# A float32 stack of two transformer blocks on one core: the gate product worked in place in PSUM, and the low weights of the split transitions made in smaller pieces and partly by VectorE

## What is computed

```
first block, layer l:
    x += norm(mix(norm(x) @ w_in) @ w_out)            # "a_in", attention, "a_out"
    x += norm((silu(h @ gate) * (h @ up)) @ down)     # h = norm(x): "a_ffn_in", "a_ffn_out"
    e = p[l] @ w_ple_up[l]                            # "a_ple_up"
    g = sigmoid(rmsnorm(x, g_ple_gate[l]) @ w_ple_gate[l])   # "a_gate"
    x += rmsnorm(e * g, g_ple_post[l])                # "a_ple"
second block, layer l:
    x += 0.5 * swiglu(norm(x)); x += mixer(norm(x)); x += 0.5 * swiglu(norm(x))
```

## Time and profile before

| | us |
|---|---|
| median of 3 runs (3408.14 to 3410.47) | 3408.16 |
| the profiled execution's own time | 3410.03 |
| its span | 3408.2 |
| TensorE busy | 3313.7 (97%) |
| GpSimd busy | 1652.4 (48%) |
| VectorE busy | 1194.6 (35%) |
| ScalarE busy | 1171.9 (34%) |
| mean granted TensorE clock, of full | 0.986 |

### The profile page before, as it was taken

One profiled execution on the slowest core, in us unless ns is written; L12 is line 12 of the kernel. 1 busy time (PEld: TensorE's weight loads), 2 busy tenths in 40 slices (PEclk: granted clock), 3 DMA queues, 4 the chain that ended last, 5 costly groups with the idle time before them and its releaser, 6 DMA issues.

```text
span 3408.2 us, 44206 instructions
## 1 busy us (share of the span) xinstructions
PE 3313.7 (97%) x16096; PEld 2741.6 (80%) x16096; DVE 1194.6 (35%) x1882; ACT 1171.9 (34%) x1848; POOL 1652.4 (48%) x894
## 2 busy tenths in 40 slices
PE   8999999999999999899999999999999999799998
PEld 6788888787788887888888788888888888588887
DVE  4534124445441144511344332124311433421133
ACT  4743222438442233422233432222322333232222
POOL 6735444567264445644447344444544453154443
PEclk9999999999999999999999999999999999899998
DMA  4112222221122222232222122222222222122221
GB/s 149 44 49 95 95 96 99 68 101 45 35 96 93 98 98 75 96 105 96 95 93 93 56 68 93 92 99 99 95 97 93 99 93 81 38 87 93 98 99 56
DMA packets 80800, 293.87 MB, mean 86 GB/s; under 512 B 8971, under 2 KB 9355, under 8 KB 80428
## 3 DMA queue, kind: packets, MB, share of 16 engines
q1 hardware_dynamic: 79344, 286.06, 25.0%
q10 hardware_dynamic: 1340, 6.23, 0.5%
HBM read 290.15 MB, written 2.10 MB: 86 GB/s over the span
## 4 chain that ended last, share of the span: by engine, by line
PE 88%; DVE 4%; POOL 4%; issue 3%; ACT 2%; DMA 0%; POOLq 0%; DVEq 0%; SPq 0%; ACTq 0%
PE bank L1953 27%; PE bank L1955 27%; PE bank L1954 27%; POOL diag L671 1%; PE bank L2375 1%; POOL scr L602 1%; POOL w_lo L556 1%; PE bank L2336 1%; PE bank L1999 1%; DVE mvl L1316 1%; PE bank L2356 1%; PE bank L1981 0%; PE bank L2198 0%; ACT w_hi L760 0%; PE bank L2176 0%
## 5 line engine op out<-in xcount | busy, mean ns | idle before, releaser
L556 POOL TENSOR_TENSOR w_lo<-w_raw,w_hi 128x1024 fp32r<-128x1024 f32 x537 | 1313.4, 2449 | 1534.4 <-ACT w_hi L760 1534.3
L1953 PE MATMUL bank<-mvh,w_hi 128*128 128x512 f32 (+1 forms) x4520 | 1745.0, 386 | 46.9 <-DVE mvl L1316 20.0
L1955 PE MATMUL bank<-mvh,w_lo 128*128 128x512 f32 (+1 forms) x4520 | 1721.1, 381 | 0.0
L1954 PE MATMUL bank<-mvl,w_hi 128*128 128x512 f32 (+1 forms) x4520 | 1720.5, 381 | 0.0
L760 ACT ACTIVATE w_hi<-w_raw 128x1024 fp32r<-128x1024 f32 x537 | 568.3, 1059 | 1774.2 <-PE bank L1955 1771.2
L1953 PEld LDWEIGHTS bank<-mvh,w_hi 128*128 128x128 f32 x4520 | 858.3, 190 | 231.8 <-issue 32.4
L1955 PEld LDWEIGHTS bank<-mvh,w_lo 128*128 128x128 f32 x4520 | 857.7, 190 | 161.6
L1954 PEld LDWEIGHTS bank<-mvl,w_hi 128*128 128x128 f32 x4520 | 858.9, 190 | 153.7 <-issue 0.2
L1394 DVE TENSOR_TENSOR scr<-bank,rstd_b 128x512 f32<-128x512 f32 x264 | 181.4, 691 | 994.3 <-PE bank L1955 994.1
L1411 DVE TENSOR_TENSOR mvl<-big,mvh 128x512 fp32r<-128x512 f32 x132 | 270.1, 2056 | 346.6 <-ACT mvh L890 346.6
L671 POOL TENSOR_TENSOR diag<-diag,scr 128x512 f32<-128x512 f32 (+1 forms) x137 | 156.2, 1140 | 23.3 <-ACT scr L785 13.1
(11 more groups left out here) (190 smaller groups left out, 1577.5 us busy)
## 6 DMA issues: line engine op xcount, KB each, us to landing
w_raw<-in_weights SPq DMA_DIRECT2D x537, 512.0 KB, 3.3
x<-in_x SPq DMA_DIRECT2D x8, 256.0 KB, 8.5
out_y<-y SPq DMA_DIRECT2D x4, 512.0 KB, 2.7
tab<-in_dist ACTq DMA_DIRECT2D x2, 640.0 KB
tab<-in_gmlp ACTq DMA_DIRECT2D x2, 640.0 KB
tab<-in_ret_dil ACTq DMA_DIRECT2D x1, 1280.0 KB
y<-in_p ACTq DMA_DIRECT2D x2, 512.0 KB, 3.4
y<-in_rotary ACTq DMA_DIRECT2D x1, 1024.0 KB
```

Of the source, the lines that this page charges most:

```text
L556: nc.gpsimd.tensor_tensor(w_lo[:, slot, :], w_raw[:, slot, :], w_hi[:, slot, :].bitcast(F32), ALU.subtract).then_inc(w_lo_ready, 1)
L1953: nc.tensor.matmul(bank[:, at], hi, mvh[:, k, at], start=first, stop=False)
L1954: nc.tensor.matmul(bank[:, at], hi, mvl[:, k, at], start=False, stop=False)
L1955: return nc.tensor.matmul(bank[:, at], lo, mvh[:, k, at], start=False, stop=last)
```

## The change

Four edits.

- **In place.** `gate_taken` scales the bank in place in PSUM, ScalarE's sigmoid works on the bank in place, and `gated` reads the bank and e. The bank is counted free by `gated`, no longer by `gate_taken`. A new semaphore, gate_scaled, tells ScalarE.
- **Order of VectorE.** Items 9 and 10 of the gate are taken one step of the x update later: scale 9 in step 0, product 9 in step 1, scale 10 in step 2, product 10 in step 3. Before all steps VectorE makes the low weights of unit 1 of the next stage (`low_weights`), in all four transitions.
- **GpSimd.** It waits for that and counts the unit with a memset of one column (`split_by_dve`). The low weights of units 2 and 3 are made in two instructions of 512 columns (`split_in_pieces`). In the gate stage the adds of squares are grouped after pairs of units, and the next stage's unit 0 is made after the root, no longer before the last adds.
- **Order of ScalarE.** After unit 5 the high weights come first; the first two pieces of x go ahead of the squares, and the later sigmoids, squares and pieces of x are interleaved anew, also in the `a_out` transitions.

```diff
--- before.py
+++ after.py
...
@@ -550,11 +550,25 @@
         @block.gpsimd
         def _(pool):
-            def split(u, slot):
+            def split(u, slot, pieces=1):
                 pool.wait_ge(w_hi_ready, u + 1)
-                nc.gpsimd.tensor_tensor(w_lo[:, slot, :], w_raw[:, slot, :], w_hi[:, slot, :].bitcast(F32),
-                                        ALU.subtract).then_inc(w_lo_ready, 1)
+                for i in range(pieces):
+                    at = slice(i * UNIT // pieces, (i + 1) * UNIT // pieces)
+                    last = nc.gpsimd.tensor_tensor(w_lo[:, slot, at], w_raw[:, slot, at],
+                                                   w_hi[:, slot, at].bitcast(F32), ALU.subtract)
+                last.then_inc(w_lo_ready, 1)
+            def split_by_dve(n):
+                pool.wait_ge(lo_by_dve, n)
+                nc.gpsimd.memset(small[:, 316:317], 0.0).then_inc(w_lo_ready, 1)
+                done[0] += 1
+            def split_in_pieces():
+                split(done[0], done[0] % RING, 2)
+                done[0] += 1
             done = [0]
@@ -684,11 +698,12 @@
                 u0, post = lin[following].u0, SPLIT_FROM
                 add_squares(name, post - 1, post + 2)
                 root(name, 0)
-                splits(u0 + 2)
+                splits(u0 + 1)
+                split_by_dve(SPLIT_POST.index(name) + 1)
                 add_squares(name, post + 3, post + 4)
-                splits(u0 + 3)
+                split_in_pieces()
                 add_squares(name, post + 4, post + 5)
-                splits(u0 + 4)
+                split_in_pieces()
                 add_squares(following, 0, 4)
                 root(name, 1)
                 add_squares(following, 4, 16)
@@ -729,10 +744,10 @@
                 splits(u0 + 4)
                 add_squares(gate, 4, KT)
                 root(gate)
-                for k in range(SPLIT_FROM):
-                    splits(u0 + RING + k)
-                    add_squares(f"a_ple{l}", max(k - 1, 0), k)
-                splits(u0 + RING + SPLIT_FROM)
+                splits(u0 + RING + 2)
+                add_squares(f"a_ple{l}", 0, 2)
+                splits(u0 + RING + RING)
+                add_squares(f"a_ple{l}", 2, SPLIT_FROM - 1)
                 second_half(f"a_ple{l}", "b_pre_in0" if l else "a_in1")
             up_to("b_mix_in0")
             retention_units()
@@ -827,20 +842,27 @@
                 k, half = SQUARES[name][i]
                 square(name, i, x[:, k, part(half)])
-            def second_half(L, taken, following, gain):
+            def second_half(L, begun, taken, following, gain):
                 i = SPLIT_FROM
+                after_unit(L, 0, i)
+                begun(i + 3)
                 taken(i + 3)
-                after_unit(L, 0, i)
+                move(following, gain, 0)
+                begun(i + 4)
+                move(following, gain, 1)
                 taken(i + 4)
-                move(following, gain, 0)
+                square_x(following, 0)
                 after_unit(L, 0, i + 1)
-                square_x(following, 0)
-                move(following, gain, 1)
                 square_x(following, 1)
+                move(following, gain, 2)
+                begun(i + 5)
+                square_x(following, 2)
+                move(following, gain, 3)
                 taken(i + 5)
                 after_unit(L, 0, i + 2)
-                for i in range(2, 16):
+                square_x(following, 3)
+                for i in range(4, 16):
                     move(following, gain, i)
                     square_x(following, i)
@@ -1164,7 +1186,7 @@
                     out_taken(i)
                 for i in range(SPLIT_FROM, KT):
                     out_taken(i)
-                second_half(L, out_taken, f"a_ffn_in{l}", f"a_pre_ffn{l}")
+                second_half(L, lambda i: None, out_taken, f"a_ffn_in{l}", f"a_pre_ffn{l}")
                 act.dma_start(y[:, 0:2, :], p_in[l]).then_inc(p_loaded, 16)
                 ffn_in(f"a_ffn_in{l}")
                 ffn_out(f"a_ffn_out{l}", f"a_ffn_in{l}")
@@ -1183,17 +1205,14 @@
                 def sigmoid(i):
                     at = part(GATE_ITEMS[i][1])
-                    act.wait_ge(bank_free, L.e0 + i + 1)
-                    nc.scalar.activation(s1[:, i % 2, at], g1[:, i % 2, at], ACT.Sigmoid).then_inc(gate_sig, 1)
+                    bank = banks[LIN[i % 4]][:, at]
+                    act.wait_ge(gate_scaled, 11 * l + i + 1)
+                    nc.scalar.activation(bank, bank, ACT.Sigmoid).then_inc(gate_sig, 1)
                 def z_taken(i):
                     k, half = GATE_ITEMS[i]
-                    act.wait_ge(z_ready, 11 * l + i + 1)
+                    act.wait_ge(bank_free, L.e0 + i + 1)
                     square(f"a_ple{l}", i, y[:, k, part(half)])
-                def gate_taken(i):
-                    sigmoid(i)
-                    z_taken(i)
                 for i in range(KT):
                     if i < SPLIT_FROM:
@@ -1203,9 +1222,9 @@
                         z_taken(i - 1)
                 z_taken(KT - 1)
                 if l:
-                    second_half(L, gate_taken, "b_pre_in0", "b_pre0")
+                    second_half(L, sigmoid, z_taken, "b_pre_in0", "b_pre0")
                 else:
-                    second_half(L, gate_taken, "a_in1", "a_pre1")
+                    second_half(L, sigmoid, z_taken, "a_in1", "a_pre1")
             for l in range(LAYERS):
                 if l:
@@ -1306,9 +1325,17 @@
                                             ALU.add).then_inc(x_ready, 1)
                 return update
+            def low_weights(u):
+                slot = u % RING
+                dve.wait_ge(w_hi_ready, u + 1)
+                nc.vector.tensor_tensor(w_lo[:, slot, :], w_raw[:, slot, :], w_hi[:, slot, :].bitcast(F32),
+                                        ALU.subtract).then_inc(lo_by_dve, 1)
             def enter_halves(name, gain, norm, update, beside):
                 L = lin[name]
+                low_weights(L.u0 + 1)
                 def low(k, half):
                     at = part(half)
@@ -1878,15 +1905,15 @@
                     else:
                         dve.wait_ge(unit_done, L.u0 + k + 1)
                     at = part(half)
-                    nc.vector.tensor_tensor(g1[:, i % 2, at], banks[LIN[i % 4]][:, at], rstd_b[:, at],
-                                            ALU.mult).then_inc(bank_free, 1)
+                    bank = banks[LIN[i % 4]][:, at]
+                    nc.vector.tensor_tensor(bank, bank, rstd_b[:, at], ALU.mult).then_inc(gate_scaled, 1)
                 def gated(i):
                     k, half = GATE_ITEMS[i]
                     at = part(half)
                     dve.wait_ge(gate_sig, 11 * l + i + 1)
-                    nc.vector.tensor_tensor(y[:, k, at], s1[:, i % 2, at], big[:, k, at],
-                                            ALU.mult).then_inc(z_ready, 1)
+                    nc.vector.tensor_tensor(y[:, k, at], banks[LIN[i % 4]][:, at], big[:, k, at],
+                                            ALU.mult).then_inc(bank_free, 1)
                 for i in range(KT):
                     gate_taken(i)
@@ -1896,14 +1923,15 @@
                 gate_taken(8)
                 variance(f"a_ple{l}", 0)
                 gated(8)
-                gate_taken(9)
                 def second_taken(k):
                     if k == 0:
+                        gate_taken(9)
+                    if k == 1:
                         gated(9)
-                    if k == 1:
+                    if k == 2:
                         gate_taken(10)
-                    if k == 2:
+                    if k == 3:
                         gated(10)
                 if l:
```

More of the change, by code:

```diff
@@ L193, in program @@
         w_loaded = [sem(f"w_loaded{i}") for i in range(RING)]
-        w_hi_ready, w_lo_ready = sem("w_hi_ready"), sem("w_lo_ready")
+        w_hi_ready, w_lo_ready, lo_by_dve = sem("w_hi_ready"), sem("w_lo_ready"), sem("lo_by_dve")
         unit_done, half_done = sem("unit_done"), sem("half_done")
@@ L211, in program @@
         p_hi, p_lo = sem("p_hi"), sem("p_lo")
-        gate_sig, z_ready = sem("gate_sig"), sem("z_ready")
+        gate_scaled, gate_sig = sem("gate_scaled"), sem("gate_sig")
         vt_done, vt_copied = sem("vt_done"), sem("vt_copied")
```

## The result

The changed kernel takes 3381.66 us, the median of 4 runs (3380.71 to 3383.26), against 3408.15 (4 runs, 3407.05 to 3410.47): a ratio of 0.9922, 95% interval 0.9907 to 0.9938. The profiled execution took 3383.26, its span is 3381.1.

A forecast was written before the change was run, and what follows sets the result against it. TensorE, busy 97%, was taken as the bound, so savings must be its idle or low-clock time. Gains of 14.2 (gate stages) and 2.4 (`a_out`) sum to 16.6 us, giving a median of 3391.5, range 3383 to 3402.

The forecast's parts named there:

- the price of the low clock behind the transitions: Low-clock loss still expected after the change: 1.0 us per transition, against 3.3 before behind the gate and 1.5 in `a_out`.
- the start race: Transition behind the gate: VectorE's and GpSimd's low weights start within 0.05 us; GpSimd first makes x updates 2 us later.
- The first rival: VectorE gets the start behind the gate and the clock never falls: 3385 us, chance 0.2.
- Gate part, gain 2.4: Gate stage before its transition: three waits worth 3.3 us go, less 0.93 of new idle, per gate stage.
- New wait 0.93: Gate unit 4: TensorE waits for unit 0's bank, now freed by the product instead of the scaling; 0.93 us new idle.
- the 1.5 for the clock behind those waits: Gate stage, 693 to 702: the lower clock following the three waits should go with them, gaining about 1.5 us.
- Transition waits, 5.3 to 3.4, gain 1.9: Transition behind the gate: new waits 0.8, 0.6, 0.6 and 1.4 us replace 5.3 us, a gain of 1.9 per gate stage.
- Four short waits will, I think, still cost one shorter stretch, 1.0: Transition behind the gate: low-clock loss falls from 3.3 us to 1.0, a gain of 2.3 per gate stage.
- Less 1.0, half the price of the start race: Deduction per gate stage for GpSimd possibly starting first, half of 2.0 us, taking 8.1 to 7.1.
- `a_out`, waits 3.8 to 3.1: `a_out` transitions: new waits of 2.6 + 0.5 us against 3.8, a gain of 0.7 each.
- it was to keep 1.0 of 1.5: `a_out` transitions: the low clock's loss shrinks from 1.5 us to 1.0, a gain of 0.5 each.
- The rule weighed: VectorE instructions with two SBUF inputs and GpSimd ones reading SBUF exclude each other; speaks against low weights on VectorE.

The follow-up runs named there:

- e3: Changed kernel with the gate product's two inputs in SBUF again and the bank free after the scaling: 3381.94 us.
- e11: Changed kernel with GpSimd's old order of adds and low weights in the gate stage: 3383.07 us.
- e13: Changed kernel with both the gate product in SBUF and GpSimd's old order in the gate stage: 3390.74 us.
- e7: Changed kernel with gate unit 4 in bank 6, otherwise idle there, instead of unit 0's bank: 3380.72 us.
- e1: Changed kernel with the low weights of units 2 and 3 in one instruction each again: 3388.61 us.
- e4: Changed kernel with one delaying memset of 1024 columns on VectorE ahead of `mvl` 1, in each transition's first half: 3381.80 us.
- e5: Changed kernel with two delaying memsets of 1024 columns on VectorE ahead of `mvl` 1, in each transition's first half: 3382.93 us.
- e8: Changed kernel with gate unit 4 in bank 6, unit 3's pieces ahead of an add, and `mvl` 1 ahead of the scaling of item 10: 3379.74 us.
- e14: Changed kernel with gate unit 4 in bank 6, unit 3's pieces ahead of an add, earlier `mvl` 1, ScalarE's old order in `a_out` only: 3378.12 us.
- e6: Changed kernel with a small memset on VectorE ahead of its low weights, so GpSimd's low weights of unit 0 start first: 3390.89 us.
- e2: Changed kernel with unit 1's low weights made by GpSimd again: 3381.62 us.
- e10: Changed kernel with ScalarE's old order in all transitions: 3392.82 us.
- e12: Kernel before the change with only the low weights of units 2 and 3 in two pieces: 3401.30 us, median of 9 runs.
- e15: Changed kernel with VectorE's old order of gate steps and ScalarE's old order in the transitions, both at once: 3392.77 us.

## Why the prediction was too high

The mechanism came out as told, and the sizes did not: the price of the low clock behind the transitions and that of the start race were paid nowhere. The first rival came about in the profiled execution: VectorE gets the start, and the clock never falls. It was given 3385 and a chance of 0.2; the median is 3.3 below that. By the steps:

- **Gate part, gain 2.4: right in size, 2.37 measured.** New wait 0.93 forecast, 0.88 measured at unit 4; the waits at units 6, 7 and the adds are gone; products 0.69. The cause was told too narrowly: the in-place product is not needed for it, nor is the order of the adds. Either will do (e3, e11, e13); with its own bank the product in place is worth 1.4 more (e7). Of the 1.5 for the clock behind those waits e13 shows 1.6.
- **Transition waits, 5.3 to 3.4, gain 1.9: mis-sized.** From start to start TensorE lost 0.7 on `mvl` 1 (0.8 forecast), 0.3 on `mvl` 2 (0.6; 697.18 - 696.78 less the usual 0.12), 0.3 on unit 2 (0.6) and 1.3 on unit 3 (1.4): 2.6, gain 2.7. `mvl` 2 (696.65) ran its free 0.48 and lost nothing to GpSimd.
- **"Four short waits will, I think, still cost one shorter stretch, 1.0": failed.** The clock is 1.00 in all four transitions. That is 1.0 per gate stage, and 1.0 per `a_out` stage, where it was to keep 1.0 of 1.5.
- **"Less 1.0, half the price of the start race": failed,** 1.0 per gate stage. VectorE won in both gate stages of the profiled execution, and in every other traced one in which the two come within 0.04 us of each other (e1, e3, e4, e5, e7, e8, e14, both stages each): a chance of one half was far off. The full price, put at 2.0, is 1.6 (e6).
- **`a_out`, waits 3.8 to 3.1: mis-sized.** 0.65 + 0.17 + 1.11 + 0.45 = 2.4. Gain 1.4 for 0.7. Of this 0.5 is a slip of the sum: its 2.6 counts from the moment TensorE could start (unit 2 at T + 10.4 and 18 matmuls of 0.12 make T + 12.6, unit 3 comes at T + 13.8: 1.2), as the gate's 3.4 does, and needs no 0.5 on top. As forecast, `mvl` 1 doesn't wait, but not thanks to VectorE's low weights: with unit 1 on GpSimd it doesn't either (e2), nor with whole instructions (e1), while with ScalarE's old order it does (0.60 in e10, 0.59 in e12). The time hangs on the pieces all the same (e1, 3.0 to 3.5).

Together 0.8 + 1.0 + 1.0 = 2.8 per gate stage (measured surplus 2.8) and 0.7 + 1.0 = 1.7 per `a_out` stage (2.2 and 1.55; the first has the 0.55 of its second half besides, for which the forecast has no term). With the measured ones, 2 x 2.8 + 3.75 = 9.4: the 25.96 of the stages less 16.6.

The gate stage's 9.9 splits by kernels: 4.0 for product or adds with their clock (e13), 4.4 for the two orders (e15), the remaining 1.5 for pieces and unit 1. The first is what the forecast had (3.9). It had not seen the second as a thing of its own: it priced the VectorE order by a tally of its steps and gave the ScalarE order no price of its own.

The rule weighed, of the Trainium skill, "SBUF — State Buffer", "Who interferes with whom", holds: 3.48 for GpSimd beside VectorE's 1.22, and 3.21 for VectorE when it came 0.27 later (e6). Its objection to this change amounts to 1.1 us on GpSimd, which nobody waited for.

**What stays open** is what decides the clock. In e14's profiled execution both gate stages have the same waits, and one has the low clock: windows over both stages, then over the stretch of the second; TensorE's rows there.

```profile
665.20:722.60 57.40, 54.24 (x419) 1.00 0.29 97
1348.60:1407.50 58.90, 55.74 (x419) 0.97 0.32 113
1379.00:1387.00 8.00, 7.80 (x53) 0.79 0.40 132
```

```profile
695.80 0.38 PE L1999 MATMUL bank<-mvh,w_hi 128*128 128x256 f32 x1 [1.73 <-DVE mvl L1359]
...
1379.20 0.39 PE L1999 MATMUL bank<-mvh,w_hi 128*128 128x256 f32 x1 [1.72 <-DVE mvl L1359]
...
1380.14 0.28 PE L2000 MATMUL bank<-mvl,w_hi 128*128 128x256 f32 x1
1380.26 0.32 PE L2001 MATMUL bank<-mvh,w_lo 128*128 128x256 f32 x1
1380.38 0.41 PE L1999 MATMUL bank<-mvh,w_hi 128*128 128x256 f32 x1
1380.60 0.41 PE L2000 MATMUL bank<-mvl,w_hi 128*128 128x256 f32 x1
```

The pitch goes from 0.12 to 0.22, from 2.4 to 1.2 GHz, some 1.2 us after the wait's end, and costs 58.78 - 57.32 = 1.46. Single waits of 1.56 (e4), 1.75 (e2) and 2.64 (e5), all for `mvl` 1, went with a lower clock in both gate stages; 1.72 and 1.73 in e8, for `mvl` 2 as in e14, and three of 1.09, 0.83 and 1.48 in e6, did not. Nor is it a matter of short waits: 0.96, 0.92 and 0.99 came before the 0.83 of e13, while 0.88, 0.55, 0.17 and 1.13 after the change came with 1.00. Nor did shorter waits mean less of it: e1's first `a_out` transition has 1.73 and 0.53 where there were 1.68 and 1.85, and the clock is 0.90 for 0.95. The length of the waits alone doesn't settle it, and a prediction can give it a chance only.

## What to carry to other kernels

Where two engines hand small pieces to each other, reorder both and price them as one edit; half of a good reordering gained nothing here, and read 0.9 to 2.2 us worse than none in the stages. Where several edits relieve the same queue, each alone can be shown to be needless: undo them together before you call any of them the cause. Read edits of 1 or 2 us from stage to stage in the trace, and price TensorE's low clock as a chance with both ends in the range, not as a fixed remainder.

## What was not expected of the hardware

- The same waits, in the same execution, with the clock at 1.00 once and at 0.79 for 8 us the next time (e14). One kernel's runs can split likewise, e12's into 3390 and 3401 with mean clocks of 0.991 and 0.988; that the low clock makes this difference too isn't shown, for no quick run of e12 was traced.
- Started within the rows' resolution (both 689.48), VectorE goes first: 1.22 for it and 3.44 to 3.48 for GpSimd in all 16 gate transitions of eight kernels where the two meet so.
- A VectorE instruction that waits for GpSimd gets in between two of GpSimd's back to back: the `mvl` of 699.21 ends at 700.71 while the two pieces run from 699.12 to 701.82, and 2.70 less a free `mvl` of 0.48 leaves 1.1 for each piece. Halving the instructions was worth 3.0 to 3.5 us per `a_out` stage (e1), and 3.55 to 4.2 by itself (e12).
- The sigmoid takes 366 ns in PSUM for 256 columns, 414 from SBUF to SBUF; VectorE's product 0.69 for 512 columns in either place when nothing holds it.
